# w_ada multiplied unsplit in f32 on two column groups, in stages that pair shift and scale columns

## The reference

```python
sc, scc = silu(c), silu(c_ctx)
shift, scale, gate = split(sc @ w_ada + b_ada, 3)        # w_ada: 2048 x 6144
shift_c, scale_c, _ = split(scc @ w_ada + b_ada, 3)
hx = rmsnorm(x, g_pre) * (1 + scale) + shift             # 512 x 2048
hc = rmsnorm(ctx, g_pre) * (1 + scale_c) + shift_c       # 256 x 2048
zx, zc = hx @ w_in, hc @ w_in[:, :XBC_W + DT_W]          # x, B, C, dt, then z, u, v, z_mlp
```

## Time and profile before

| | before |
|---|---|
| runs, median of 3 | 2802.37 us |
| profiled execution | span 2803.5 us; no other time is given for it |
| TensorE busy | 2755.5 us, 98% |
| VectorE, ScalarE, GpSimd busy | 1539.7, 1124.7, 331.9 us |
| front (to the first unit of the third block) | 0 to 168.44 us |
| first early tile | 58.51 us |

### The profile page before, as it was taken

The page is one execution under the profiler, slowest core; times in us unless marked ns, Lnnn a source line. Parts: engine busy times, 40 slices in busy tenths (PEclk is TensorE's granted clock), DMA queues, the critical chain, the costliest instruction groups (busy, mean ns, idle before and its releaser), DMA issues. The chain is left out here.

```text
span 2803.5 us, 33298 instructions
## 1 busy us (share of the span) xinstructions
PE 2755.5 (98%) x13110; PEld 2243.4 (80%) x13110; DVE 1539.7 (55%) x1862; ACT 1124.7 (40%) x1484; POOL 331.9 (12%) x409
## 2 busy tenths in 40 slices
PE   6999999999999999999999999899999999999999
PEld 2688888878888888888888888788888888788787
DVE  6867678674555546666753233544445544533733
ACT  7742222234343333333332332436656553442611
POOL 1011100000334124322311000100000000000000
PEclk8999999999999999999999999999999999999999
DMA  9647767654455554455455333242222223223252
GB/s 398 242 171 271 245 249 276 234 213 145 143 167 175 163 177 149 152 177 188 143 170 209 110 119 105 84 142 84 89 76 83 83 83 109 86 90 98 97 181 91
DMA packets 162122, 439.35 MB, mean 157 GB/s; under 512 B 14768, under 2 KB 59824, under 8 KB 151728
## 3 DMA queue, kind: packets, MB, share of 16 engines
q1 hardware_dynamic: 123360, 307.28, 33.0%
q0 software_dynamic: 15792, 92.99, 9.4%
q10 hardware_dynamic: 22816, 36.97, 3.7%
HBM read 398.11 MB, written 39.06 MB: 156 GB/s over the span
## 5 line engine op out<-in xcount | busy, mean ns | idle before, releaser
L1641 DVE TENSOR_TENSOR WL<-RAW,WH 128x1024 fp32r<-128x1024 f32 (+1 forms) x424 | 516.3, 1226 | 745.0 <-ACT WH L1009 574.7
L414 PE MATMUL PB<-HH,WH 128*128 128x512 f32 x2048 | 816.8, 399 | 5.0 <-DVE WL L1641 3.8
L419 PE MATMUL PB<-HL,WH 128*128 128x512 f32 x2048 | 802.0, 392 | 0.0
L420 PE MATMUL PB<-HH,WL 128*128 128x512 f32 x2048 | 801.9, 392 | 0.0
L1009 ACT ACTIVATE WH<-RAW 128x1024 fp32r<-128x1024 f32 (+1 forms) x424 | 433.6, 1038 | 442.7 <-PE PB L527 257.4
L525 PE MATMUL PB<-WH,HH 128*128 128x512 f32 x1248 | 490.5, 393 | 1.6 <-ACT Kr L1009 0.8
L527 PE MATMUL PB<-WH,HL 128*128 128x512 f32 x1248 | 486.6, 390 | 0.0
L526 PE MATMUL PB<-WL,HH 128*128 128x512 f32 x1248 | 486.4, 390 | 0.0
L414 PEld LDWEIGHTS PB<-HH,WH 128*128 128x128 f32 x2048 | 385.2, 188 | 93.4 <-issue 10.8
L419 PEld LDWEIGHTS PB<-HL,WH 128*128 128x128 f32 x2048 | 386.2, 189 | 65.5 <-issue 3.3
L420 PEld LDWEIGHTS PB<-HH,WL 128*128 128x128 f32 x2048 | 385.6, 188 | 66.0
(11 more groups left out here) (324 smaller groups left out, 2704.3 us busy)
## 6 DMA issues: line engine op xcount, KB each, us to landing
RAW<-in_w_in_t SPq DMA_DIRECT2D x320, 512.0 KB, 3.7
AU<-in_w_ada POOLq DMA_DIRECT2D x64, 1024.0 KB, 5.5
RAW<-in_w_out_t SPq DMA_DIRECT2D x96, 512.0 KB, 3.7
bcb<-R SPq DMA_DIRECT2D x64, 256.0 KB, 6.3
S<-so ACTq DMA_DIRECT2D x24, 384.0 KB, 2.4
ebc<-R SPq DMA_DIRECT2D x32, 256.0 KB, 6.0
SY<-evb ACTq DMA_DIRECT2D x32, 256.0 KB, 2.6
yin<-SY POOLq DMA_DIRECT2D x32, 256.0 KB, 4.0
```

The source lines that it names most:

```text
L414: h.matmul(banks[j], lh, m.HH[:, t, :], start=st, stop=False)
L419: h.matmul(banks[j], lh, m.HL[:, t, :], start=False, stop=False)
L420: ins = h.matmul(banks[j], ll, m.HH[:, t, :], start=False, stop=en)
L1641: return h.tensor_tensor(o, a, b, op)
```

## The change

The product with w_ada is no longer split. scs is an f32 tile of 32 columns for each 128 rows, of which 2 are filled and 30 are zero; the moving operand is the unit as it landed. The two 512-column halves of a unit (its two groups of 128 rows) go to two column groups of 32 (partitions r to r + 31 of bank 5), so the fold sums them: it is 4 f32 matmuls over 64 partitions of rowb by a selection matrix `sel`. Stages alternate between partitions 0 to 63 and 64 to 127. A stage now holds 256 shift and the same 256 scale columns, so each stage makes Am for 2 channel tiles, and turns come in twos every four beats. Early tiles begin in beat 7 and there are 39 beats, not 42; a stage's four tiles are 2 channel tiles by 2 blocks. The x tiles are loaded behind the first six w_ada units, and the squares and scalings of x stand ahead of ScalarE's and VectorE's loops. Three more places (in WH[0], WH[2], WL[0]) hold w_ada units, a place is freed by "a used", and early weights have four half-slots in WH/WL[3] and WH/WL[1]. RAW units stand in the list ahead of the units of `RAW_AT`.

```diff
@@ -108,10 +108,21 @@
 NUNIT = AT_OUT2 + UNITS_OUT2


-ADA_ORDER = (0, 4, 1, 5, 2, 6, 3, 7)
-
-PLACE = list(range(16)) + [16, 17, 18, 19, 22, 23] + list(range(6, 14)) + [20, 21] + \
-    [14, 15, 16, 17, 18, 19, 22, 23, 12, 13, 20, 21, 14, 15, 16, 17] + [18, 19, 22, 23, 20, 21] * 2 + [18, 19, 22, 23]
+def places():
+
+
+    last = [9, 17, 9, 17, 9, 9, 25, 33, 25, 33, 25, 25, 41, 49, 41, 49, 41, 41, 57, 63, 57, 63, 57, 57, 63, 63, 63]
+    used = [-1] * 27
+    out = []
+    for i in range(64):
+        j = min((j for j in range(27) if last[j] >= i), key=lambda j: (used[j], last[j], j))
+        used[j] = i
+        out.append(j)
+    return out
+
+
+PLACE = places()
+RAW_AT = (10, 12, 20, 28, 34, 38, 44, 52)
 BLOCKS = (0, 12) + tuple(range(1, 12)) + (13, 14, 15)
 EARLY = 8

@@ -119,24 +130,30 @@
 def beat(k):


-    st = None
-    if 8 <= k <= 32 and k % 8 == 0:
-        st = k // 4 - 1
-    elif 6 <= k < 32 and k % 8 == 6:
-        st = (k - 2) // 4 - 1
-    p, r = divmod(k - 9, 8)
-    t = 4 * p + r if k >= 9 and r < 4 and p < 4 else None
-    return st, t, k - 10 if 10 <= k < 10 + 4 * EARLY else None
-
-
-BEATS = 10 + 4 * EARLY
+    st = k // 4 - 1 if k % 4 == 0 and 4 <= k <= 32 else None
+    p, r = divmod(k - 5, 4)
+    t = 2 * p + r if k >= 5 and r < 2 and p < 8 else None
+    return st, t, k - 7 if 7 <= k < 7 + 4 * EARLY else None
+
+
+BEATS = 7 + 4 * EARLY


 def early_tile(s):

-    u, tt = divmod(s, 4)
-    return u, BLOCKS[u % 2], tt, 4 * (u // 2) + tt
-
+    st, r = divmod(s, 4)
+    return 2 * st + r // 2, r // 2, 2 * st + r % 2, r % 2
+
+
+def early_half(e):
+
+    st, b = divmod(e, 2)
+    return 2 * (st // 2) + b, slice(st % 2 * 512, st % 2 * 512 + 512)
+
+
+def early_slot(e):
+
+    return (3, 1)[e % 4 // 2], slice(e % 2 * 512, e % 2 * 512 + 512)


 AWAIT_V = (8, 0)
@@ -227,13 +244,15 @@
     m.xs = [at(f"xs{i}", WA + 8 * KB * i, [128, 2048]) for i in range(6)]
     m.hf = [at(f"hf{i}", WA + 48 * KB + 3 * KB * i, [128, 768]) for i in range(2)]
     m.rowb = at("rowb", WA + 54 * KB, [128, 512])
-    m.scs = at("scs", WA + 56 * KB, [128, 16, 4], F32R)
+    m.scs = at("scs", 132 * KB, [128, 16, 32])
     m.junk = at("junk", 56 * KB, [128, 2048])
     m.aus = []
...
         for nm, off in (("HH", 8 * q), ("HH", 8 * q + 4), ("HL", 32 + 8 * q), ("HL", 36 + 8 * q), ("CH", 64 + 4 * q),
...


     o = WA
@@ -425,27 +444,26 @@

     def a_unit(i):
         st, kk = divmod(i, 8)
-        bank = reuse(5) if kk == 0 else PB[5]
         P.wait_ge(*at("scs"))
-        P.wait_ge(*at("a hi", i))
-        P.wait_ge(*at("a lo", i))
+        P.wait_ge(*at("aus", i))
+        if kk == 0 and st >= 2:
+            P.wait_ge(*at("rowb", st - 2))
         for j in range(2):
-            for part in (m.WH[i % 3], m.WL[i % 3]):
-                ins = h.matmul(bank[0:4, :], m.scs[:, 2 * kk + j, :], part[:, j * 512:(j + 1) * 512],
-                               start=kk == 0 and j == 0 and part is m.WH[i % 3],
-                               stop=kk == 7 and j == 1 and part is m.WL[i % 3])
+            r = 64 * (st % 2) + 32 * j
+            ins = h.matmul(PB[5][r:r + 32, :], m.scs[:, 2 * kk + j, :], m.aus[PLACE[i]][:, j * 512:(j + 1) * 512],
+                           start=kk == 0, stop=kk == 7)
         ins.then_inc(*put(s.unit, "a used", i))
-        freed[5] = [("rowb", st)]

     def fold(st):
         P.wait_ge(*at("rowb", st))
         P.wait_ge(*at("cst"))
         if st:
             P.wait_ge(*at("mod", st - 1))
-        if st >= 2:
-            P.wait_ge(*at("hc", 4 * (st // 2) - 1))
+            P.wait_ge(*at("hc", 2 * st - 1))
+        r = slice(64 * (st % 2), 64 * (st % 2) + 64)
         for j in range(4):
-            ins = h.transpose(PB[7][:, 256 + 4 * j:260 + 4 * j], m.rowb[0:4, j * 128:(j + 1) * 128], ident[0:4, 0:4])
+            ins = h.matmul(PB[7][:, 256 + 2 * j:258 + 2 * j], m.rowb[r, j * 128:(j + 1) * 128], m.C("sel")[r, :],
+                           start=True, stop=True)
         ins.then_inc(*put(P.side, "fold", st))

     def turn(t):
@@ -483,16 +501,18 @@
...
         if sub is not None:
-            u, b, tt, t = early_tile(sub)
-            P.wait_ge(*at("g hi", u, tt // 2))
-            P.wait_ge(*at("g lo", u, tt // 2))
+            e, i, t, r = early_tile(sub)
+            P.wait_ge(*at("g hi", e))
+            P.wait_ge(*at("g lo", e))
             first_h(t)
-            tk = early[u % 2]
-            ins = t_tile(m.WH[3][:, tt * 256:(tt + 1) * 256], m.WL[3][:, tt * 256:(tt + 1) * 256], t,
-                         [tk[0][1], tk[1][1]], tk[2][1] if b < 12 else None)
-            if tt % 2:
-                ins.then_inc(*put(s.unit, "g used", u, tt // 2))
-    freed[6], freed[7] = [("hx", 15)], [("hc", 15)]
+            tk = early[i]
+            w, half = early_slot(e)
+            cols = slice(half.start + r * 256, half.start + r * 256 + 256)
+            ins = t_tile(m.WH[w][:, cols], m.WL[w][:, cols], t, [tk[0][1], tk[1][1]],
+                         tk[2][1] if BLOCKS[i] < 12 else None)
+            if r:
+                ins.then_inc(*put(s.unit, "g used", e))
+    freed[5], freed[6], freed[7] = [("rowb", 7)], [("hx", 15)], [("hc", 15)]


     fine = deque()
@@ -1025,62 +1045,49 @@
...
-    A.then(act(m.scs[:, :, 0:2], m.scv, ACT.Copy), "scs hi")
+    A.wait_ge(*at("scs zero"))
+    A.then(act(m.scs[:, :, 0:2], m.scv, ACT.Copy), "scs")

...
-        i = max(i for i in range(64) if PLACE[i] == j)
-        A.wait_ge(*at("a hi", i))
-        A.wait_ge(*at("a lo", i))
-
-    def a_high(i):
-        A.wait_ge(*at("aus", i))
-        if i >= 3:
-            A.wait_ge(*at("a used", i - 3))
-        act(m.WH[i % 3], m.aus[PLACE[i]], ACT.Copy).then_inc(*put(s.hi, "a hi", i))
+        A.wait_ge(*at("a used", max(i for i in range(64) if PLACE[i] == j)))

...
-    def early_high(sub):
-        u, b, tt, t = early_tile(sub)
-        half = slice(tt * 256, tt * 256 + 512)
+    def early_high(e):
+        u, half = early_half(e)
+        w, place = early_slot(e)
         A.wait_ge(*at("raw", u))
-        if u:
-            A.wait_ge(*at("g used", u - 1, tt // 2))
-        act(m.WH[3][:, half], m.RAW[u % 3][:, half], ACT.Copy).then_inc(*put(s.hi, "g hi", u, tt // 2))
+        if e >= 4:
+            A.wait_ge(*at("g used", e - 4))
+        act(m.WH[w][:, place], m.RAW[u % 3][:, half], ACT.Copy).then_inc(*put(s.hi, "g hi", e))

     junk = None
-    a_high(0)
-    a_high(1)
+    for v in range(6):
+        A.wait_ge(*at("x", v))
+        if junk:
+            A.wait_ge(*junk)
+        junk = A.then(act(m.junk, m.xs[v], ACT.Square, acc=m.ss[:, v:v + 1]), "x squared", v)
     for k in range(BEATS):
         t = beat(k)[1]
-        for i in (2 * k, 2 * k + 1):
-            if t is not None and i % 2:
-                modulate(t)
-            if i + 2 < 64:
-                a_high(i + 2)
-            if 3 <= i < 15 and i % 2:
-                v = (i - 3) // 2
-                A.wait_ge(*at("x", v))
-                if junk:
-                    A.wait_ge(*junk)
-                junk = A.then(act(m.junk, m.xs[v], ACT.Square, acc=m.ss[:, v:v + 1]), "x squared", v)
+        if t is not None:
+            modulate(t)
         sub = beat(k + 2)[2]
         if sub is not None and sub % 2 == 0:
-            early_high(sub)
+            early_high(sub // 2)
     make(8)
@@ -1662,46 +1669,35 @@
...
-    V.wait_ge(*at("scs hi"))
-    V.then(TT(m.scs[:, :, 2:4], m.scv, m.scs[:, :, 0:2].bitcast(F32), ALU.subtract), "scs")
+    V.then(h.memset(m.scs, 0.0), "scs zero")
...
-    def a_low(i):
-        V.wait_ge(*at("aus", i))
-        V.wait_ge(*at("a hi", i))
-        if i >= 3:
-            V.wait_ge(*at("a used", i - 3))
-        TT(m.WL[i % 3], m.aus[PLACE[i]], m.WH[i % 3].bitcast(F32), ALU.subtract).then_inc(*put(s.lo, "a lo", i))
+        V.wait_ge(*at("a used", max(i for i in range(64) if PLACE[i] == j)))

     def rows_out(st):
+        r = slice(64 * (st % 2), 64 * (st % 2) + 64)
         V.wait_ge(*at("a used", 8 * st + 7))
-        if st:
-            V.wait_ge(*at("fold", st - 1))
-        V.then(h.tensor_copy(m.rowb[0:4, :], m.PB[5][0:4, :]), "rowb", st)
+        if st >= 2:
+            V.wait_ge(*at("fold", st - 2))
+        V.then(h.tensor_copy(m.rowb[r, :], m.PB[5][r, :]), "rowb", st)
+
+    modp = m.mod.rearrange("p (s t j) -> p s t j", s=2, j=2)
+    b_ada = m.P("b_ada").rearrange("p (s t) -> p s t", s=2)

...
     def finish(st):
-        c = 4 * ADA_ORDER[st]
-        sums = m.PB[7][:, 256:272].rearrange("p (t j) -> p t j", j=4)
+        c = slice(2 * st, 2 * st + 2)
         V.wait_ge(*at("fold", st))
         V.wait_ge(*at("par"))
-        t = V.then(TT(m.modv[:, c:c + 4, :], sums[:, :, 0:2],
-                      m.P("b_ada", c, 4).unsqueeze(2).to_broadcast([128, 4, 2]), ALU.add))
+        t = V.then(TT(modp[:, :, c, :], m.PB[7][:, 256:264].rearrange("p (s t j) -> p s t j", s=2, j=2),
+                      b_ada[:, :, c].unsqueeze(3).to_broadcast([128, 2, 2, 2]), ALU.add), "mod", st)
```

(72 more changed lines are left out.)

## The result

| | before | after |
|---|---|---|
| runs, median | 2802.4 us (6 runs) | 2813.31 us (6 runs, 2809.3 to 2816.26) |
| ratio, 95% interval | | 1.0039 (1.0028 to 1.005) |
| profiled execution | span 2803.5 | 2811.88, span 2810.1 |
| first early tile | 58.51 | 44.05 |
| end of the front | 168.44 | 178.89 |

The change makes the kernel slower by 10.9 us, 0.39%. The forecast was 2807 us with a range of 2793 to 2820.

The account below looks back on a forecast made before the run. TensorE, 98% busy, bounds the kernel, with the feed deciding until the first tile. First tile 44.2, list to 166.0, waits 4.6 + 1.3 and clock 1.5 give 173.4 against 168.44: +5.0, 2807 us, range 2793 to 2820.

Parts of the forecast that it names:

- case A: Whole kernel: the forecast's own sum holds, 2807 us, own range 2803 to 2811; chance 0.33.
- case B: Unit blocks: passes queue within a column group, each block's tail costing 0.32 us more; 2816.5 us, slower; chance 0.26.
- Loads and start: Start of front: unit 15 lands at 42.9 us, first early tile at about 44.2 us, 14.3 sooner.
- A unit and a beat without a turn: TensorE's front list: a unit costs 0.854 us, a block 0.36 more; beat without a turn 2.07, before 1.86.
- Case D: Unit matmuls: all four passes run together, 20.5 us less, waits 4 more; 2790 us; chance 0.12.
- A turned beat: TensorE's front list: turn 0.36, unit 1.10, context turn 0.14, unit 1.21; 2.81 us, before 2.50.
- The fold: Eight stages: 4 f32 matmuls replace 4 transposes, priced from L540 at 0.81 plus 0.10, 0.91 us each.
- The gates: Load queue: RAW(7) delays unit 52, TensorE waits 4.6 us; RAW(5) delays units 38 and 39, 0.9 and 0.4.
- The half clock: Behind the load waits: an idle stretch lets TensorE's clock fall, adding 1.5 us, between 0 and 3.
- Behind the front: After the front: nothing changes but its start; unit 9's slot comes free 8 us before it is read.

Follow-up runs that it names:

- experiment 3: Changed kernel with both halves of a unit in the same 32 columns, so one column group; 2852.61 us, 1.0174 of before.
- experiment 1: Changed kernel with RAW(5), RAW(6), RAW(7) moved to stand ahead of w_ada units 42, 48, 58, not 38, 44, 52; 2801.87 us, 0.9995 of before.
- experiment 2: Changed kernel with both turns first in a turned beat, then both units in one block; 2813.98 us, 1.0035 of before.
- Experiment 7: Changed kernel with load gates moved, one block per beat, fold by transposes, and w_in unit 9 split later; 2794.88 us, 0.9967 of before.
- experiment 5: Changed kernel with both the load gates moved and each turned beat's units in one block; 2798.41 us, 0.9986 of before.
- experiment 8: Changed kernel with RAW(7) alone moved, from ahead of unit 52 to ahead of unit 58; 2805.27 us, 1.0008 of before.

## Why the forecast came out as it did

The forecast named slower as likelier than faster, its range held the time, and every mechanism of case A is in the trace. But the time lies above case A's own range (2803 to 2811); the wider range held it by the room that it gave to case B, which the traces rule out. The forecast fell 6 us short: 2.6 in the price of turned beats and folds, 2.9 at the gates, 0.9 behind the front.

**Loads and start: right.** First tile at 44.2 forecast, 44.05 measured. The count of loads at 1.27 us each was enough.

**A unit and a beat without a turn: right.** 2.07 forecast, 2.03 measured. Case B, passes that queue within a group, would have given 2816.5, near what was measured, and is still wrong: there is no tail of 0.43 us behind a pair of units, only 0.10 us (0.96 for the second unit against 0.88 for the first) and what the tile bears. The view of one tile of after, a single unit, has its four passes start within 0.4 us, two at 61.07 and two at 61.50, each 0.59 long (min, median, max in ns, then first and last start in us):

```profile
L453 PE MATMUL PB<-aus21HL,scs x4: 592/592/592, 61.1 to 61.5; 128*32 128x512 f32 x4
```

Four passes one behind the other would take 1.7 us, as experiment 3 shows them. Case D (2790) needs all four at once and would make a unit 0.43; it takes 0.88. The Trainium skill's strict order of starts and ends (TensorE: Matmul & The Clock Gate, Part 3), which the forecast set beside case B, holds in these rows and brings no tail. A total that fits is no evidence for a mechanism; the per-step view is.

**A turned beat: 2.81 forecast, 2.97 measured.** The units cost less than the step said (0.98, and 0.98 + 0.11, against 1.10 and 1.21), but the turns cost more: 0.53 and 0.37 against 0.36 and 0.14. The step gave the mode's price to the units alone and let the transposes keep their old durations. They pay too, mostly in their last step: from the last transpose to the unit's start it is 0.20 us in after, where before has 0.03; and the first of the two context transposes, behind a unit, takes 0.17 us instead of 0.11. In 12 beats 1.9 us.

**The fold: 0.91 forecast, 1.08 measured.** L540 has the same instructions, but stands between other neighbours and streams one column: its first step is 0.03 us where the fold's is 0.13, its last 0.11 against 0.18, and the steps between are 0.11 in both. In 7 folds 1.2 us. These two terms, less 0.5 for the beats without a turn, are 2.6 us: the list without waits was put at 166.0 us (its terms as written add up to 166.1), and experiment 1, which has none, ends its front at 168.50.

**The gates: 7.4 us forecast, 10.3 measured.** The wait at unit 52 was right (4.6 forecast, 4.25 measured; turn to issue 4.5 forecast, 4.4 measured). The one at unit 38 was mis-sized: 0.9 + 0.4 forecast, 2.47 + 0.27 measured. The step let its unit land 9.2 us after the turn; it landed at 11.3, because the load took 6.5 us from issue and not 3.4 + 1.27. Five more units are issued right behind it (93.64 to 96.51) and may share the DMA engines with it; but so it is at unit 52, which took 4.4. Experiments 2 and 3 have both gates and the same difference (7.3 and 5.9 us against 4.4 and 4.4), so it is no chance of one execution. In after the issue of unit 38 itself took 1.48 us, that of unit 52 0.43, and in the 4.4 us behind the issue the DMA engines moved 220 GB/s at the one and 308 at the other. Why they differ stays open, so the good fit at unit 52 is in part luck. The half clock cost 3.3 us in the two together, against 1.5 taken and a bound of 3.

**Behind the front: "nothing changes" was wrong by 0.9 us.** The step had unit 9 free 8 us before it is read. What counts is not its reader but what stands behind its split on ScalarE and VectorE: the first block's convolution, for which TensorE waits next. Experiment 7 shows it.

**Sum:** 173.4 + 2.6 + 2.9 = 178.9 for the end of the front, and 178.89 was measured. With 0.9 behind the front that is 11.35 us at the mark, against 10.9 between the medians. The forecast took before's span of 2803.5 us as 1.1 over its median; in time that execution was some 2.9 over, as said above. No term of the sum hung on it. The medians agree with the mark to half a microsecond, which is luck in part: the runs of after spread over 7 us.

**What the change was worth.** Without the gates it gains nothing (experiment 1), since six more units behind the first tile and dearer folds and blocks take what the early start and the fuller stretch to 40 us bring. With one block for each beat, the fold by transposes and unit 9 later it gains 7.6 us.

## What to carry to other kernels

In a queue that issues in order, a load that waits for a late event holds all behind it. Put it where the event plus a full landing on an empty queue (here 4.4 to 7.3 us) still lies ahead of the reader of the next load; moving three entries of a list was worth 11.4 us. Price a short block in another mode by its neighbours too, and on both sides; gather such blocks. And an edit that makes the engine earlier shows nothing while a gate stands behind it (experiments 2 and 5): take the gate away first.

## What was not expected

- Two column groups of 32 columns halve f32 matmuls of 512 columns almost exactly: 0.88 us a unit with two, 1.74 with one.
- A wait of 2.7 to 4.3 us on TensorE costs 1.5 to 1.8 us more behind it, and the clock falls late: in after it goes to its lower level (1.2 GHz of 2.4) only when TensorE works again (at 99.7 and 137.2 us), in experiment 8 at 98.9, half a microsecond before. A unit takes 1.85 us at it where it takes 0.96 otherwise.
- One load out of a dry queue lands in 4.4 us and its like in 5.9 to 7.3 us, each at the same place of the list in three or four kernels.
